# Last expert's rows kept in SBUF and placed by a 0/1 product; the other rows fetched and partly summed under it

## The chip, the cores and the metric

One core of a Trainium2 chip runs the whole program. The metric is the device time of one execution in microseconds (us), the median of several. A profile is one further execution with the hardware profiler on; its own time stands beside it. TensorE is PE in the profile, VectorE is DVE, ScalarE is ACT, GpSimd is POOL and SyncE is SP.

## The reference, cut to what matters

A trunk of two layers over 1024 tokens of width 1024, all in float32. Each layer has an attention mixer, a residual with layer norm, and then a mixture of experts with its own residual and layer norm. What matters here is the second half:

```python
g_sel = argmax(g_logits)                       # one group of 8 experts of 32
top_val, top_idx = lax.top_k(e_logits, 2)      # two experts in the group
weights = g_gate * softmax(top_val)
# each (token, expert) pair:
h = silu(xb @ w_gate[e]) * (xb @ w_up[e])      # 1024 -> 512, twice
out = h @ w_down[e]                            # 512 -> 1024
y = segment_sum(out * row_w, row_tok)          # two weighted rows a token
x = layer_norm(ALPHA * x + y, gain, bias)      # ALPHA = 4 ** 0.25
```

Every token has two pairs, so there are 2048 expert rows of 4 KB in a layer.

## The kernel before, in words

Tokens lie in 8 tiles of 128 (one token a partition). The program is five blocks: attention of layer 0, experts of layer 0, attention of layer 1, experts of layer 1, and a last one. At the end of a block all engines meet at a barrier, and GpSimd clears the semaphores of the block that has ended. `Block()` is opened in `open_block`.

**Experts** (`Moe.run`). A block of 128 slots is computed for each of the 32 experts, one after the other. For expert `e`, GpSimd gathers the tokens' rows by an indirect DMA (`gather`, L1698), TensorE turns them, and three products follow: gate, up, down. Each is made of three passes of fp32r products (high part by high part, low by high, high by low), so the 2 MB of each weight matrix is split by ScalarE into a high part (L1848) and by VectorE into a low part (L352). `Moe.run`'s functions `step` hold one expert's work for each engine, and the engines work through them in order. The result goes from PSUM banks 6 and 7 to `res` (L1881 on ScalarE, L1953 on VectorE), and GpSimd sends it by an indirect DMA (`scatter`, L1703) to `o_dram` (`expert_rows`), where a token's two rows lie side by side. An expert with more than 128 tokens would have further blocks (`extra_blocks`, `more`); with these inputs there are none (64 gathers and 64 scatters in all), but what finds them out is computed: `plan_extras` at expert 30, `mark_extras` on VectorE at expert 31, `list_extras` on TensorE behind the last down product, and `keep_extras` on VectorE behind that. Only then do the engines test the count. Behind its last scatter's landing, and behind that test, GpSimd gives `rows_sent`, and SyncE fetches tile 0's rows (`first_rows`).

**Sum and norm** (`Combine`). For layer 0 it is the opening of the next attention block, for layer 1 a block of its own. For a tile `t` SyncE fetches the first rows (L2007) and the second rows (L2008), 512 KB each; it holds four tiles and asks for `t` when tile `t-2` has landed (`sync`). The rows x1 (the residual) are fetched earlier, under the last expert (L1995), four tiles of them in layer 0 and all eight in layer 1. Then:

- ScalarE scales the first rows by their weight into PSUM (L2072).
- VectorE adds the second rows with their weight (L2081), and then ALPHA times x1 (L2086).
- VectorE takes the moments (L989 to L992), ScalarE a square root (L997), VectorE the scale (L1002, L1003), ScalarE normalises (L1009).
- GpSimd multiplies by the gain (L1013) and adds the bias (L1017).
- SyncE writes the tile (L2059). In layer 1 tile 7 doesn't go through GpSimd: VectorE does its gain and bias (L2099, L2103).

In layer 0, VectorE and ScalarE first split three weight slices of the next attention (`split_w`). TensorE turns each finished tile (L343), ScalarE and VectorE split the turned tile (`keep_tile`: L348, L352), and TensorE starts the attention's projections (`first_halves`, L643) when tiles 0 to 3 have been kept; tiles 4 to 7 and the other halves follow. Matrices of plain float32 are multiplied nowhere in `Combine`; `ident` is a 128x128 float32 identity, used for turning.

## Time and profile before

| what | value |
|---|---|
| runs | 2459.29, 2459.82, 2468.2 us; median 2459.82 |
| the profiled execution's own time | 2462.13 us |
| its span in the profile | 2460.4 us |
| mean granted TensorE clock | 0.961 of 2.4 GHz |
| PE busy | 2277.2 us (93%) |
| DVE busy | 1797.3 us (73%) |
| ACT busy | 1363.2 us (55%) |
| POOL busy | 248.0 us (10%) |

Busy shares are of the span. The 1.7 us between span and time lie around the first and the last recorded instruction. TensorE's clock has two levels here, 1.2 and 2.4 GHz, which the profile writes as 0.50 and 1.00. In the page's 40 slices, counted from 0, TensorE is busy 9 tenths or more in nearly all. The low ones are slice 18 (1107 to 1168 us, the end of layer 0's experts and the opening of its sum and norm, 4 tenths), slice 19 (7 tenths) and slice 39 (2398 to 2460 us, the sum and norm of layer 1, 0).

### The profile page before, as it was taken

Reading aid. Unit: us, or ns where it says so; the run is one execution under the profiler, and the core shown is the slowest. Engines: PE = TensorE matmul, PEld = TensorE weight load, DVE = VectorE, ACT = ScalarE, POOL = GpSimd, SP = SyncE. Lnnn points to the kernel's source line nnn. Section 1 sums busy time; section 2 is a strip of 40 time slices with the busy share of each in tenths; the row PEclk is TensorE's granted clock in tenths of the full one; section 3 lists DMA queues with packets and bytes.
Section 4 is the critical chain, followed back from the end, with each engine's and each line's share of the span. In section 5 each row is a group of like instructions: output and inputs, shape, how many; then the busy total and the mean of one; then the engine's idle time right before and its main releaser. Section 6 shows DMA issues by size and latency. Waiting matters only on the chain. (4 is left out here: it accounts for less than half of the span.)

```text
span 2460.4 us, 33859 instructions
## 1 busy us (share of the span) xinstructions
PE 2277.2 (93%) x12788; PEld 1873.8 (76%) x12788; DVE 1797.3 (73%) x2520; ACT 1363.2 (55%) x1662; POOL 248.0 (10%) x238
## 2 busy tenths in 40 slices
PE   8999998989999999994799999989989999999990
PEld 6767886878888888883678778867778888888870
DVE  4665556568999999996555555556579999999986
ACT  3454435026777777773344444443047777777753
POOL 0000000001111111111400000000011111111105
PEclk9999999989999999996899999999999999999995
DMA  4010004229999999997311111105069999999975
GB/s 130 24 30 27 27 15 143 86 99 368 391 378 383 382 385 384 386 356 251 138 46 37 37 37 38 37 35 183 26 230 405 392 400 392 385 381 373 376 283 209
DMA packets 155146, 534.31 MB, mean 217 GB/s; under 512 B 39232, under 2 KB 79192, under 8 KB 105832
## 3 DMA queue, kind: packets, MB, share of 16 engines
q1 hardware_dynamic: 136208, 498.45, 53.9%
q0 software_dynamic: 18432, 33.60, 3.6%
q8 instruction: 105, 1.72, 0.3%
q14 instruction: 57, 0.47, 0.1%
q10 hardware_dynamic: 344, 0.08, 0.0%
HBM read 515.21 MB, written 50.39 MB: 230 GB/s over the span
## 5 line engine op out<-in xcount | busy, mean ns | idle before, releaser
L352 DVE TENSOR_TENSOR arena<-arena,arena 128x2048 fp32r<-128x2048 f32 (+1 forms) x458 | 955.2, 2116 | 76.9 <-ACT arena L1848 56.6
L1848 ACT CAST arena<-arena 128x2048 fp32r<-128x2048 f32 x384 | 716.1, 1917 | 134.9 <-PE psum L1625 120.1
L1625 PE MATMUL psum<-arena,arena 128*128 128x512 f32 x3072 | 734.2, 395 | 0.0
L1625 PEld LDWEIGHTS psum<-arena,arena 128*128 128x128 f32 x3072 | 569.6, 189 | 114.6 <-issue 0.4
L643 PE MATMUL psum<-arena,arena 128*128 128x512 f32 x2016 | 506.0, 401 | 8.3 <-DVE arena L352 7.6
L643 PEld LDWEIGHTS psum<-arena,arena 128*128 128x128 f32 x2016 | 369.7, 189 | 102.0 <-issue 16.2
L1636 PE MATMUL psum<-arena,arena 128*128 128x512 f32 x1536 | 365.1, 394 | 2.8 <-DVE arena L352 2.8
L1636 PEld LDWEIGHTS psum<-arena,arena 128*128 128x128 f32 x1536 | 291.6, 190 | 66.5 <-DVE arena L352 4.3
L352 DVE TENSOR_TENSOR arena<-psum,arena 128x512 fp32r<-128x512 f32 (+1 forms) x186 | 161.2, 874 | 106.3 <-ACT arena L768 55.2
L785 ACT ACTIVATE arena<-arena,arena 128x640 f32<-128x640 f32 (+4 forms) x192 | 120.0, 626 | 202.8 <-DVE arena L883 152.3
L343 PE MATMUL psum<-ident,arena 128*128 128x128 f32 x1024 | 151.0, 289 | 64.3 <-POOL arena L1017 26.7
L343 PEld LDWEIGHTS psum<-ident,arena 128*128 128x128 f32 x1024 | 145.6, 196 | 81.2 <-POOL arena L1017 31.6
L1168 PE MATMUL psum<-arena,arena 128*128 128x512 f32 x768 | 194.7, 410 | 8.5 <-ACT arena L348 6.8
L737 ACT COPY arena<-psum 128x512 f32<-128x512 f32 (+3 forms) x288 | 119.8, 467 | 116.9 <-PE psum L674 116.3
L1168 PEld LDWEIGHTS psum<-arena,arena 128*128 128x128 f32 x768 | 148.7, 198 | 40.8 <-issue 7.2
L1698 POOL DMA_INDIRECT arena<-x_rows,slot_rows x64 | 97.9, 1530 | 505.8 <-DMA expert_rows<-arena,slot_rows 437.6
L674 PE MATMUL psum<-ident,arena 128*128 128x128 f32 x888 | 131.0, 277 | 16.1 <-ACT arena L737 10.9
L674 PEld LDWEIGHTS psum<-ident,arena 128*128 128x128 f32 x888 | 105.7, 141 | 44.8 <-ACT arena L737 14.7
L696 PE MATMUL psum<-arena,arena 128*64 128x128 f32 x1776 | 127.2, 283 | 0.0
L883 DVE CUSTOM_DVE_ANT_0 arena<-psum,arena 128x640 f32<-128x640 f32 (+3 forms) x192 | 104.9, 572 | 28.1 <-PE psum L662 27.7
L1703 POOL DMA_INDIRECT expert_rows<-arena,slot_rows x64 | 63.9, 998 | 545.2 <-DVE arena L1953 520.4
L662 PE MATMUL psum<-arena,arena 64*128 64x320 f32 (+5 forms) x1056 | 114.6, 336 | 2.5 <-DVE arena L883 1.3
(166 smaller groups left out, 1548.4 us busy)
## 6 DMA issues: line engine op xcount, KB each, us to landing
arena<-in_moe_w_gate SPq DMA_DIRECT2D x128, 1024.0 KB, 8.5
arena<-in_moe_w_up SPq DMA_DIRECT2D x128, 1024.0 KB, 7.7
arena<-in_moe_w_down SPq DMA_DIRECT2D x128, 1024.0 KB, 6.9
arena<-expert_rows SPq DMA_DIRECT2D x32, 512.0 KB, 5.3
x_rows<-arena SPq DMA_DIRECT2D x24, 512.0 KB, 2.7
arena<-x_rows SPq DMA_DIRECT2D x24, 512.0 KB, 7.2
arena<-in_c_w_in SPq DMA_DIRECT2D x24, 512.0 KB, 4.2
arena<-in_x SPq DMA_DIRECT2D x16, 512.0 KB, 7.3
```

The lines of the kernel that those rows point to most:

```text
L343: m = pe.transpose(dst_bank[:, j * P:(j + 1) * P], rows[:, c0 + j:rows.shape[1]:stride], ident[:])
L352: return eng.tensor_tensor(tile, src, high.bitcast(F32), ALU.subtract)
L643: mm = pe.matmul(job_bank(i, g), w[:, c * P:(c + 1) * P], xs[:, c, half_cols(g)], start=(a == 0), stop=(a == 23))
L662: done[h] = pe.matmul(psum[:, at:at + w], qs[b][own, t * P:(t + 1) * P], ks[kv][own, k0 + a:k0 + a + w], start=(k == 0), stop=(k == 2))
L674: mm = pe.transpose(bank(B_TURN + h)[:, (b - 4 * g) * P:(b - 4 * g + 1) * P], probs_of(s, h)[:, b * P:(b + 1) * P], ident[:])
L696: mm = pe.matmul(bank(B_OUT)[DH * h:DH * (h + 1), (t % 4) * P:(t % 4 + 1) * P], v_r[pair.kv][:, (kt + b) * P + DH * h:(kt + b) * P + DH * ...
L737: copy(probs_t[s % 2][h][:, a:b], bank(B_TURN + h)[:, 0:b - a]).then_inc(t_copied[h], 1)
L785: act.activation(probs_a[s % 2][h][:, 0:ahead + nk], biased[h][:, 0:ahead + nk], ACT.Exp, bias=low[s % 2][h], scale=-1.0, accum_out=rowsum ...
L1168: return pe.matmul(bank(2 * (t % 2) + half), ys[:, c, t * P:(t + 1) * P], w[:, c, half * BANK:(half + 1) * BANK], start=(k == 0 and c == 0 ...
L1625: mm = pe.matmul(bank(o), cs[:, c * P:(c + 1) * P], ws[:, c * FF:(c + 1) * FF], start=(k == 0 and c == 0), stop=(k == 2 and c == CH - 1))
L1636: mm = pe.matmul(bank(B_Y + s), hs[:, c * P:(c + 1) * P], ws[:, c * D + s * BANK:c * D + (s + 1) * BANK], start=(k == 0 and c == 0), stop= ...
L1848: act.copy(w_hi[w][:, cols], self.raw[w][:, cols]).then_inc(hi_ready[w], 1)
```

## The change

Seven things are altered, in both layers unless said.

1. **The last expert's rows stay.** Expert 31's result is not copied to `res` and not scattered. ScalarE multiplies each half of it, straight from PSUM, by the weight of each slot (`w_slot`) into `tail_hi` (fp32r), and VectorE forms `tail_lo`, the product less the high part. The first half is released by the down product before its second half (`half_done`).
2. **A 0/1 matrix a tile.** `pick_tokens` (VectorE, at expert 30) writes `picks`: for a slot of expert 31 and a token, 1 where the token is the slot's.
3. **Weights by slot.** The 2048 pair weights are written to DRAM at expert 6 (`w_dram`), and one indirect DMA (behind expert 10's scatter) fetches those of expert 31's slots. `clear_last` fills expert 31's rows in `o_dram` with zeros at the start.
4. **Rows are fetched under the last expert.** SyncE fetches tiles 0 to 6 from when expert 30's rows have landed, each into a place of its own. Tile 7's follow when the last expert's rows are in `tail`. In layer 0 the residual's tiles 4 to 7 come behind those.
5. **Sums ahead.** Under the last down product, ScalarE scales the first rows of tiles 0 to 2 and VectorE finishes tiles 0 and 1 (rows and residual); tile 2 is finished in the next block.
6. **TensorE adds.** `sum_up(t)`: `picks` by `tail_hi` and `tail_lo` for every tile, and for tiles 3 to 7 before that the identity by the first and by the second rows, both scaled by ScalarE and both plain float32. Layer 1 has four pairs of banks for it, layer 0 two. VectorE then has one addition of 1024 columns a tile instead of two.
7. **Around it.** `Block(no_gpsimd_drain=True)`. The extra blocks are found out only where the count isn't zero. The square root's table is loaded at the end of the experts. In layer 1 tile 3 too is ended on VectorE. In layer 0 the three weight slices are split inside the loop over tiles.

The core of the diff (what is left out names semaphores, moves buffers, and rewrites the extra blocks, which don't run here):

```diff
-            return ctx2.enter_context(nc.Block())
+            return ctx2.enter_context(nc.Block(no_gpsimd_drain=True))
...
+                            if half_done is not None and k == 2 and s == 0:
+                                mm.then_inc(half_done, 1)
...
                     for e in range(EXPERTS - 2):
+                        if e == 6:
+                            sp.wait_ge(before.weights_ready, 1)
+                                sp.dma_start(w_dram.rearrange("(t p k) o -> p k (t o)", p=P, k=2), w_pair[:]
+                                             ).then_inc(w_sent, 16)
...
+                    sp.wait_ge(lo_ready[UP], 1 + 2 * EXPERTS)
+                    combine.rows_ahead(sp, 0)
+                    sp.wait_ge(y_out[0], 8 * EXPERTS)
+                    sp.wait_ge(y_out[1], 8 * EXPERTS)
+                    sp.wait_ge(xt_ready, 1 + EXPERTS)
+                    combine.fetch_rows(sp, 0)
+                    sp.wait_ge(up_done, 1 + EXPERTS - 1)
+                    combine.fetch_rows(sp, 1)
+                    sp.wait_ge(up_done, 1 + EXPERTS)
+                    combine.fetch_rows(sp, 2)
+                    sp.wait_ge(gate_done, 1 + EXPERTS)
+                    combine.fetch_rows(sp, 3)
+                    sp.wait_ge(lo_ready[DOWN], 1 + 2 * EXPERTS)
+                    combine.rows_ahead(sp, 1)
+                    for t in range(4, TILES - 1):
+                        combine.fetch_rows(sp, t)
...
+                    sp.wait_ge(tail_lo, 2)
+                    combine.last_rows(sp)
...
+                    def clear_last():
+                        pool.memset(res[1], 0.0).then_inc(cleared, 1)
+                        pool.memset(w_slot, 0.0).then_inc(cleared, 1)
+                        pool.wait_ge(cleared, 2)
+                        scatter(res[1], slot_rows[:, LAST, 1:2], y_out[1])
...
-                        act.wait_ge(down_done, 1 + e + 1)
                         act.wait_ge(res_free, e + 1)
-                        act.copy(res[b][:, 0:BANK], bank(B_Y)).then_inc(y_act, 1)
+                        if not last:
+                            act.wait_ge(down_done, 1 + e + 1)
+                            act.copy(res[b][:, 0:BANK], bank(B_Y)).then_inc(y_act, 1)
+                            return
+                        combine.scale_first(act, 0)
+                        combine.scale_first(act, 1)
+                        act.wait_ge(x_rows_in, 16)
+                        for s in range(2):
+                            act.wait_ge(down_done, ALL_DOWN - 1 + s)
+                            act.mul(tail[0][:, s * BANK:(s + 1) * BANK], bank(B_Y + s), w_slot).then_inc(tail_hi, 1)
+                        combine.scale_first(act, 2)
...
+                    act.activation(stats[:, 0, 19:20], ident[:, 0:1], ACT.Sqrt)
...
                             before.plan_extras(dve)
+                            pick_tokens()
                         else:
-                            before.mark_extras(dve)
+                            count.append(extra_count(dve))
+                            combine.make(dve, 0)
+                            combine.make(dve, 1)
...
+                        for s in range(2):
+                            cols = slice(s * BANK, (s + 1) * BANK)
+                            dve.wait_ge(tail_hi, s + 1)
+                            dve.scalar_tensor_tensor(out=tail[1][:, cols], in0=bank(B_Y + s), scalar=w_slot,
+                                                     in1=tail[0][:, cols].bitcast(F32), op0=ALU.mult,
+                                                     op1=ALU.subtract).then_inc(tail_lo, 1)
...
+                    def pick_tokens():
+                        chain.link(dve.tensor_copy(last_token, slot_rows[:, LAST, 0:1]))
+                        chain.link(dve.tensor_scalar(token_in, tile_from[:], last_token, None, ALU.add))
+                        for t in range(TILES):
+                            dve.tensor_scalar(picks[:, t * P:(t + 1) * P], iota_cols[:], token_in[:, t:t + 1], None,
+                                              ALU.is_equal)
...
+                whole = (3, TILES - 1) if last else ()
+                write_order = (0, 1, 3, 2, 4, 5, 7, 6) if last else range(TILES)
+                    return bank(2 * (t % 4), 2) if last else bank(2 + 2 * (t % 2), 2)
...
-                def scale_first(act, t):
-                    self.rows_here(act, t)
-                    if t >= 2:
-                        act.wait_ge(added, t - 1)
-                    act.mul(sum_banks(t), firsts[t % 4], w_pair[:, 0, t:t + 1]).then_inc(scaled, 1)
+                def sum_up(pe, t):
+                    if t >= pairs_of_banks:
+                        pe.wait_ge(added, t - pairs_of_banks + 1)
+                    if t >= MADE:
+                        self.was_scaled(pe, t)
+                    pick = self.picks[:, t * P:(t + 1) * P]
+                    for s in range(2):
+                        cols = slice(s * BANK, (s + 1) * BANK)
+                        into = sum_banks(t)[:, cols]
+                        if t >= MADE:
+                            pe.matmul(into, ident[:], firsts[t][:, cols], start=True, stop=False)
+                            pe.matmul(into, ident[:], seconds[t][:, cols], start=False, stop=False)
+                        pe.matmul(into, pick, self.tail_hi[:, cols], start=(t < MADE), stop=False)
+                        mm = pe.matmul(into, pick, self.tail_lo[:, cols], start=False, stop=True)
+                    mm.then_inc(summed, 1)
...
-                    if not last:
-                        for i in range(3):
-                            split_w(i)
-                    scale_first(act, 0)
+                    self.scale_both(act, 3)
+                    self.scale_both(act, 4)
                     for t in range(TILES):
-                        if t + 1 < TILES:
-                            scale_first(act, t + 1)
                         if t >= 1:
                             act_norm(act, t - 1)
+                        if 1 <= t < TILES - 4:
+                            self.scale_both(act, t + 4)
+                        if not last and t in (1, 2):
+                            split_w(t - 1)
...
-                    for t in range(4):
+                    for t in range(3):
                         turn_tile(t)
+                        sum_up(pe, t + 5)
+                    turn_tile(3)
                     first_halves(0)
```

How instructions stand now, at the places that matter. SyncE behind its last weights, in layer 1, before (numbers of `arena` are places in SBUF; the first eight here hold the residual's tiles):

```order
L1670 DMA arena_72<-in_ln_gain 128x1024
L1670 DMA arena_72<-in_ln_bias 128x1024
L1995 DMA arena_19082<-x_rows 128x1024
...
L1995 DMA arena_19089<-x_rows 128x1024
L1598 TENSOR_LOAD plan
```

and after:

```order
L2126 DMA arena_19226<-x_rows 128x1024
L2138 DMA arena_19199<-expert_rows 128x1024
L2139 DMA arena_19207<-expert_rows 128x1024
...
L2138 DMA arena_19202<-expert_rows 128x1024
L2139 DMA arena_19210<-expert_rows 128x1024
L2126 DMA arena_19227<-x_rows 128x1024
L2126 DMA arena_19228<-x_rows 128x1024
L2126 DMA arena_19229<-x_rows 128x1024
L2126 DMA arena_19230<-x_rows 128x1024
L2138 DMA arena_19203<-expert_rows 128x1024
L2139 DMA arena_19211<-expert_rows 128x1024
```

Fourteen fetches of rows have come in front of the test of the count: those of tiles 0 to 3 between the residual's two halves, those of tiles 4 to 6 behind them.

VectorE from expert 30's end to the last expert's end, in layer 1, after (19233 is `picks`, 19199 to 19201 are the first rows of tiles 0 to 2, 19207 and 19208 the second rows, 19223 and 19224 the residual, 19231 and 19232 `tail_hi` and `tail_lo`):

```order
L2074 TENSOR_SCALAR arena_19233<-iota_cols,arena_19292 128x128 x8
L2058 COPY arena_19282<-psum 128x512
L357 TENSOR_TENSOR arena_19195<-arena_19189,arena_19192 128x2048 x2
L2037 TENSOR_TENSOR arena_19285<-arena_19284,psum 128x512
L357 TENSOR_TENSOR arena_19287<-psum,arena_19286 128x512
L1614 TENSOR_LOAD plan
L1614 ISA x2
L2178 SCALAR_TENSOR_TENSOR arena_19199<-arena_19207,w_pair,arena_19199 128x1024
L2183 SCALAR_TENSOR_TENSOR arena_19199<-arena_19223,arena_19199 128x1024
L2178 SCALAR_TENSOR_TENSOR arena_19200<-arena_19208,w_pair,arena_19200 128x1024
L2183 SCALAR_TENSOR_TENSOR arena_19200<-arena_19224,arena_19200 128x1024
L2065 SCALAR_TENSOR_TENSOR arena_19232<-psum,arena_19290,arena_19231 128x512 x2
```

The picks stand in front of the copy of expert 30's result, and four passes over tiles 0 and 1 stand where `mark_extras` was, in front of the low part of the tail.

TensorE in the last block, where it had nothing before (tile 2's four products, then tile 3's first half; 19202 and 19210 are tile 3's rows):

```order
L2259 MATMUL psum<-arena_19231,arena_19233 128x512
L2260 MATMUL psum<-arena_19232,arena_19233 128x512
L2259 MATMUL psum<-arena_19231,arena_19233 128x512
L2260 MATMUL psum<-arena_19232,arena_19233 128x512
L2257 MATMUL psum<-arena_19202,ident 128x512
L2258 MATMUL psum<-arena_19210,ident 128x512
L2259 MATMUL psum<-arena_19231,arena_19233 128x512
L2260 MATMUL psum<-arena_19232,arena_19233 128x512
```

Tiles 0 to 2 have four products each, tiles 3 to 7 eight, half of them by the float32 identity.

## Rows read from the trace of the kernel before

**Rows 1.** The timeline, layer 1's end: start us, length, engine, line, count.

```profile
2380.21 0.69 DVE L1953 COPY arena<-psum 128x512 f32<-128x512 f32 x1
2381.74 0.97 POOL L1703 DMA_INDIRECT expert_rows<-arena,slot_rows  x1 [16.18 <-DVE arena L1953]
2382.81 4.49 DVE L352 TENSOR_TENSOR arena<-arena,arena 128x2048 fp32r<-128x2048 f32 x2 [1.91 <-ACT arena L1848]
2390.11 8.66 PE L1636 MATMUL psum<-arena,arena 128*128 128x512 f32 x24 [1.40 <-DVE arena L352]
2400.33 0.97 POOL L1703 DMA_INDIRECT expert_rows<-arena,slot_rows  x1 [17.62 <-DVE arena L1953]
2404.43 0.32 SPq L2007 DMA_DIRECT2D arena<-expert_rows  x1
2410.09 1.12 ACT L2072 ACTIVATE psum<-arena,w_pair 128x1024 f32<-128x1024 f32 x1 [10.70 <-PEq L2214]
2410.44 0.42 SPq L2008 DMA_DIRECT2D arena<-expert_rows  x1
```

**Rows 2.** The chain of work that ended last: start us, length, what.

```profile
2411.80 6.50 DMA arena<-expert_rows
2422.83 2.35 POOL arena L1013
2453.63 2.38 POOLq L2214
```

**Rows 3.** The timeline, one tile's work in layer 1's last block.

```profile
2428.65 1.22 DVE L2086 SCALAR_TENSOR_TENSOR arena<-arena,psum 128x1024 f32<-128x1024 f32 x1
2430.23 1.24 ACT L1009 ACTIVATE arena<-arena,stats 128x1024 f32<-128x1024 f32 x1 [2.02 <-DVE stats L1003]
2431.38 1.10 ACT L2072 ACTIVATE psum<-arena,w_pair 128x1024 f32<-128x1024 f32 x1
2431.74 1.28 DVE L2081 SCALAR_TENSOR_TENSOR psum<-arena,w_pair,psum 128x1024 f32<-128x1024 f32 x1
2433.05 1.22 DVE L2086 SCALAR_TENSOR_TENSOR arena<-arena,psum 128x1024 f32<-128x1024 f32 x1
```

**Rows 4.** Windows of layer 1's end: stretch, length, busy of five engines, PEclk, DMA share, GB/s.

```profile
2384.00:2388.00 4.00, 1.34 (x7) 0.80 (x5) 3.90 (x3) 0.59 (x1) 0.00 (x0) 1.00 0.07 26
2416.00:2420.00 4.00, 0.00 (x0) 0.00 (x0) 2.51 (x2) 1.92 (x3) 0.00 (x0) 0.50 1.01 409
```

**Rows 5.** The timeline, end of layer 0 and opening of layer 1's attention.

```profile
1144.96 2.94 ACT L756 CAST arena<-arena 128x1024 fp32r<-128x1024 f32 x3 [10.88 <-PEq L2214]
1176.34 1.22 DVE L2086 SCALAR_TENSOR_TENSOR arena<-arena,psum 128x1024 f32<-128x1024 f32 x1
1182.18 1.22 DVE L2086 SCALAR_TENSOR_TENSOR arena<-arena,psum 128x1024 f32<-128x1024 f32 x1
1186.94 7.81 PE L643 MATMUL psum<-arena,arena 128*128 128x512 f32 x24 [4.49 <-DVE arena L352]
1212.18 16.61 PE L643 MATMUL psum<-arena,arena 128*128 128x512 f32 x72 [1.55 <-DVE arena L352]
```

**Rows 6.** The timeline, products by the float32 identity (two records each).

```profile
528.40 3.15 PE L1122 MATMUL psum<-ident 128*128 128x128 f32 x26
544.36 4.62 PE L1122 MATMUL psum<-ident 128*128 128x128 f32 x20
```

**Rows 7.** Windows of 1 us, PE alone: busy, PEclk, DMA share, GB/s.

```profile
1175.00:1176.00 1.00, 1.00 (x7) 0.50 1.04 426
2395.00:2396.00 1.00, 1.00 (x4) 0.50 0.02 8
```

**Rows 8.** Groups by form, 0/1 rows on VectorE: count | busy, mean ns.

```profile
L1390 DVE TENSOR_SCALAR arena<-iota_cols,arena 128x128 f32<-128x128 f32 x32 | 9.0, 283 | 0.3
```

**Rows 9.** The DMA view, 405 to 420 us: packets, and an issue's size and landing.

```profile
DMA packets 6164, 2.68 MB, mean 179 GB/s; under 512 B 5552, under 2 KB 5552, under 8 KB 6162
```

**Rows 10.** Waits, 600 to 1100 us: total, times, longest.

```profile
ACT arena L1848 <- PE psum L1625: 56.5, 56, 1.3
```

308 lines of the change are left out of this document (205 added, 103 removed).

## The prediction, made before the changed kernel ran

> **What bounds the kernel now.** I read the page's busy slices first. They show TensorE nearly full everywhere but at the two sums and norms, so a change there counts in full, and one under the experts counts only where it delays TensorE. The waits of the expert stage say the same: ScalarE's weight splits wait for TensorE, not for a DMA [rows 10].
>
> Then the timeline of layer 1's end [rows 1]. The last down product ends at 2398.8, the last scatter is issued at 2400.3, the first fetch of rows follows 4.1 us later, and ScalarE starts the last block at 2410.1. The chain of waits [rows 2] goes through the landing of tile 2's rows at 2418.3 to GpSimd, which starts at 2422.8 and then never stops: it ends its seventh tile at 2456.0, 33.2 us later, 4.74 a tile. The last write lands with the span's end, 4.4 us behind. So the end is set by when GpSimd starts, how many tiles it has, and whether it must pause.
>
> Layer 0's end is the same 1265.1 us earlier (1144.96 against 2410.09) [rows 1, 5], but there VectorE has most to do, a tile in 5.84 us (its second additions at 1176.34 and 1182.18). TensorE's first projection waits for VectorE until 1186.9, and the attention proper starts at 1212.2 [rows 5].
>
> **The change part by part.**
>
> *Under the experts.* The picks are 8 instructions of 0.283 us [rows 8] and two small ones of some 0.2: 2.6 us in front of the copy at 2380.21, which then ends at 2383.5. The low split of the last down weights behind it began at 2382.81 [rows 1], so the last expert gets 0.7 us later, in each layer. Expert 30's scatter moves from 2381.7 to 2384.3. The zero fill and the weights' fetch stand on GpSimd, idle for most of an expert (16 to 17 us ahead of a scatter) [rows 1]; I take them at nothing. The 2048 weights of 4 bytes go by SyncE's queue at expert 6. The nearest row is the router's load: 5552 packets under 512 B within some 15 us, along with larger ones [rows 9], so 2048 need at most 6 us of a queue, and nobody waits for a DMA there. I take 0.3 us for both layers; the bounds are 0 and 6 each.
> The Trainium skill (DMA: Bandwidth & Descriptors, Specifications) says that below 512 B the DMA engine does a read-modify-write. No row here shows a 4-byte write; by that rule I would sooner go to the upper bound.
>
> *Rows under the last expert.* Moved past on SyncE's queue: the residual's second half (layer 0: two weight slices) now stands behind tiles 0 to 3 and behind the wait for expert 30's scatter, which ends after the other waits there. Its first reader is tile 4's addition, over 30 us later, so I count nothing. Fetches start at 2384.3 + 4.1 = 2388.4, into a DMA that is all but idle (share 0.07 in 2384 to 2388) [rows 4]. A tile's pair of 1.05 MB takes 2.6 us at the 409 GB/s of a full queue [rows 4]; 2.7 taken. Tile 2's pair landed 6.5 us from issue with another ahead of it [rows 2], which leaves 1.3 of start-up. Tile 0 lands at 2388.4 + 0.9 (issue) + 1.3 + 2.6 = 2393.2, tile 3 at 2401.3, and tile 4, behind the residual's 2 MB, at 2409.4. Tiles 0 and 1 are scaled and made (1.10, then 1.28 + 1.22 each [rows 3]) by 2399.4, beside the down product, which ends at 2399.5; the tail's low part then ends at 2401.
>
> *The barrier.* TensorE's listing of extra blocks, the last scatter and its landing go. Before, 5.7 us passed from SyncE's start of the first fetch to ScalarE's first work behind the barrier (2404.43 to 2410.09) [rows 1]. With no GpSimd drain I take under 1 us behind the last engine, which is ScalarE: tail's high part 2400.1, tile 2's scaling 2401.2, test of the count, table and root 1.5 us; the block opens at 2404.0. Bounds: 2403, and 2409.5 if the whole 5.7 us stays. In layer 0, SyncE has four fetches more and I take 1139.6.
>
> *Layer 1.* GpSimd's start now needs tile 0's root, which on ScalarE stands behind the scaling of tile 4: 2409.4 + 2 x 1.1 = 2411.6, root 0.2, VectorE's scale 0.4, normalise 1.24 [rows 3], with gaps 2414.0 (before 2422.8). Three tiles take it to 2428.2. Now VectorE is late: ScalarE's rounds of 4.2 us (2 x 1.1, 0.2, 1.24 and VectorE's scale between) give tile 3's root at 2424, two passes of 1.28 end it at 2426.7, and moments of tile 4, addition of tile 5 and tile 4's scale and normalise bring tile 4 to GpSimd at 2431.5: a pause of 3.3. Three more tiles: 2445.7 against 2456.0, a gain of 10.3.
>
> *TensorE's additions.* A float32 identity product of 128 columns is two records: 26 in 3.15 us at 2.4 GHz and 20 in 4.62 at 1.2 [rows 6], so 0.24 and 0.46 us. Of 512 columns none is in the trace. Bounds: the price of an fp32r product, 0.23 (16.61 / 72) [rows 5], and four times 0.24. I take four times, 0.97, since the record's length goes with columns; a tile of 3 to 7 then costs 4 x 0.97 + 4 x 0.23 = 4.8 us at 2.4 GHz and 9.2 at 1.2. In layer 1 four pairs of banks let TensorE run on from tile 0 without a stop, so it is at the high level within tile 3 (in [rows 1] 24 products took 8.66 from a low start) and ends each tile before VectorE asks.
> The Trainium skill (FP8 and Floating Point Precision, TensorE Precision Notes) has true FP32 as four passes; the trace agrees (0.24 against 0.06 for a quarter of 0.23).
>
> *Layer 0.* TensorE's turns of tiles 0 to 3 and the projections now queue behind the sums of tiles 4 to 7, and these behind VectorE's additions two tiles back. VectorE loses 1.28 a tile and gets the three splits (1.2 each) inside the loop, where ScalarE has 2.2 us of scaling and 1.05 of splitting in the first rounds. Laying the four engines' programs against each other by hand with the durations above, the additions of tiles 0 to 7 end at 1143.4, 1146.5, 1153.9, 1161.3, 1168.3, 1173.0, 1179.3, 1184.0. Before, tile 7's was at 1189.2 (1182.18 + 5.84 + 1.22) [rows 5]. The start of the block gains 5.4, and what the loop gains and pays cancels out; the gain handed to the attention is 5.2.
>
> *Sum.* -10.3 - 5.2 + 0.3, and 1 us for engines that load code behind the jump over the extra blocks (unseen; 0 to 5.7, the barrier's bound) = -14.2. The profiled execution's 2462.1 (span 2460.4 and 1.7 around it) becomes 2447.9. It stood 2.3 above the median, so for the median 2459.8 - 14.2 = 2445.6.
>
> **The rivals.**
>
> *The barrier stays long.* The profile puts the release down to TensorE, not GpSimd [rows 1, 5]. For it: the releaser. Against it: the two layers' 5.7 and 5.6 us fit an end of GpSimd's own. Blocks open at 2409.5 and 1145.1: layer 1 gains 6, layer 0 nothing, in all 2454.
>
> *DMA is slower.* Up to nine tiles' worth are queued at once. At 3.4 us a pair tile 4 lands 5 us later: 5.3 and 2.3 gained, 2452.5. Against it stands the 409 GB/s.
>
> *Layer 0's clock swings.* There two pairs of banks make TensorE wait for VectorE at every tile. If it falls to 1.2 GHz in each gap, a tile costs some 7 us and layer 0 gains 1: 2449.7. For it: brief work in gaps stayed at 0.50 (1175) [rows 7]. Against: the new work fills over three quarters of the time.
> The Trainium skill (TensorE: Matmul & The Clock Gate, A second HAM failure mode: psum-queue depth-cycling) describes just that, small idle times between groups that cycle through banks; by it the sum is 2449.7.
>
> *Slower.* TensorE stays at 1.2 GHz through all additions, as it did in layer 0's turns [rows 7]. At 9.2 us a tile it passes GpSimd's 4.74 and VectorE's round, and the sum of tile 7 sets both ends: by the same timetables layer 0 ends 7.3 and layer 1 4.5 later than before, with the 1.3 above 2473. It turns slower once a tile costs over 7.9 us in both layers. Against: in [rows 1, 7] solid work of 6 us raised the clock (0.50 still at 2395, the 24 products over in 8.66 where all at 1.2 GHz would need over 10).
>
> *It does not do what it says* (the landings come too late for the sums ahead, and tail and barrier wait for them): only with a pair over 4 us; 2457.
>
> *Everything fits.* 2.56 us a pair, full clock from tile 3 in layer 0: 11.2 and 7.7, 2441.
>
> **How the numbers follow.** Forecast 0.50; barrier 0.12, DMA 0.09, swinging clock 0.10, slower 0.05, too late 0.04, everything fits 0.10. Time 2445.6, the forecast's own range 2443 to 2449. The range 2440 to 2455 leaves out the slow case and the worst ends. A measurement of this kernel can tell about 0.5% from no change, 12.3 us, so "faster" begins at 2447.5. Of the forecast three quarters lie below (0.38), all of "everything fits" (0.10), and 0.06 of the others: 0.54. Slower 0.06, same 0.40.
>
> **What would show it.** In the profile after: the last down product 0.7 us later; rows fetched from about 10 us ahead of its end; 3 to 5 us from it to the last block's first work; GpSimd's first gain at 2414 less layer 0's 5, six tiles with a pause of some 3 us in the middle; float32 products of some 0.43 us a record at 2.4 GHz; layer 0's addition of tile 7 some 5 us earlier. Wrong would be: a block that opens more than 7 us behind the down product, VectorE's additions waiting for TensorE in layer 1, PEclk at 0.50 beyond tile 4 in either layer, or expert rounds longer than before.

## The result: 0.4% slower, and the profile after

| | before | after |
|---|---|---|
| median of 12 runs each, beside one another | 2462.38 us | 2471.69 us |
| lowest, highest | 2457.28, 2468.2 | 2469.94, 2476.17 |
| profiled execution, its span | 2462.13, 2460.4 | 2471.77, 2469.8 |

The ratio is 1.0041, with a 95% interval of 1.0031 to 1.0050. By the bound of 0.5% in the prediction this is "the same"; by the interval it is slower. The 2445.6 forecast is missed by 26 us, and the range (to 2455) by 17.

I compared the traces stage by stage, by the start of GpSimd's scatters and of TensorE's products. The two run together to within 0.3 us up to expert 5's scatter in layer 0 (673.31 and 673.20). Then:

| stretch | shift at its end | made in it | predicted |
|---|---|---|---|
| layer 0, experts 6 and 7 (scatter 1082.09, now 1089.59) | +7.5 | +7.5 | +0.15 |
| layer 0's end (attention proper 1212.18, now 1222.55) | +10.4 | +2.9 | -5.2, code +1 |
| attention of layer 1 (a scatter 1884.70, now 1896.99) | +12.3 | +1.9 | 0 |
| layer 1, experts 6 and 7 (2364.58, now 2384.28) | +19.7 | +7.4 | +0.15 |
| layer 1's end (span) | +9.4 | -10.3 | -10.3 |

So layer 1's end came out as forecast, and the loss lies in three places where I had counted nothing or a gain: the two stalls (14.9 where I had 0.3), layer 0's end (2.9 where I had -4.2) and the attention (1.9 where I had 0). Together that is 23.6 us, the whole miss of the span (+9.4 for -14.2).

**Where the experts stall.** First SyncE's queue in the timeline of after, at expert 6 (start us, length, line), then ScalarE and TensorE:

```profile
661.76 0.65 SPq L1690 DMA_DIRECT2D pair_weights<-w_pair  x1
664.18 6.65 SPq L1566 DMA_DIRECT2D arena<-in_moe_w_up  x2
670.88 6.75 SPq L1566 DMA_DIRECT2D arena<-in_moe_w_gate  x2
...
682.68 1.90 ACT L1929 CAST arena<-arena 128x2048 fp32r<-128x2048 f32 x1 [4.65 <-DMA arena<-in_moe_w_up]
...
681.51 2.10 PE L1645 MATMUL psum<-arena,arena 128*128 128x512 f32 x8
689.00 7.53 PE L1656 MATMUL psum<-arena,arena 128*128 128x512 f32 x24 [5.39 <-DVE arena L357]
```

The two pairs of issues behind the write, which took 3.17 and 2.53 us at this place in before, take 6.65 and 6.75; I read that as a queue that takes no more. ScalarE now waits for a DMA there, where [rows 10] showed it waiting for TensorE alone, and TensorE stands still for 5.4 us and restarts at the low clock (PEclk 0.50 from 688 to 692). The windows of before and after (last two columns: DMA share, GB/s) show what the queue carried:

```profile
668.00:672.00 4.00, 4.00 (x23) 3.45 (x22) 4.00 (x3) 2.27 (x4) 0.00 (x0) 1.00 0.99 410
672.00:676.00 4.00, 4.00 (x19) 3.30 (x18) 2.98 (x3) 4.00 (x3) 1.00 (x1) 1.00 1.01 419
676.00:680.00 4.00, 4.00 (x20) 3.30 (x19) 4.00 (x4) 3.25 (x3) 0.00 (x0) 1.00 1.00 370
```

```profile
668.00:672.00 4.00, 4.00 (x23) 3.45 (x22) 4.00 (x3) 2.23 (x4) 0.00 (x0) 1.00 0.89 61
672.00:676.00 4.00, 4.00 (x20) 3.28 (x19) 2.94 (x3) 2.59 (x2) 1.00 (x1) 1.00 0.54 36
676.00:680.00 4.00, 4.00 (x19) 3.34 (x18) 2.85 (x2) 1.91 (x1) 0.00 (x0) 1.00 0.78 139
684.00:688.00 4.00, 0.00 (x0) 0.00 (x0) 2.29 (x1) 2.74 (x3) 1.48 (x1) 0.74 1.02 427
```

In these 12 us the queues moved 3.9 MB less than in before, about 9.4 us at 410 GB/s. TensorE is still full while the rate is low (column 3). Its gap opens at 683.6, some 15 us after the rate fell and 3 after it had recovered, which is why the cause has to be looked for ahead of the stall.

**Layer 0's end.** The timeline of after, SyncE's queue, ScalarE, GpSimd, VectorE and TensorE:

```profile
1135.13 6.23 SPq L314 DMA_DIRECT2D arena<-in_c_w_in  x2
1141.40 3.39 SPq L2138 DMA_DIRECT2D arena<-expert_rows  x1
1149.40 2.54 SPq L2126 DMA_DIRECT2D arena<-x_rows  x4
...
1152.45 4.27 ACT L2156 ACTIVATE arena<-arena,w_pair 128x1024 f32<-128x1024 f32 x4 [7.44 <-PEq L2421]
...
1160.95 2.37 POOL L1023 TENSOR_TENSOR arena<-arena,arena 128x1024 f32<-128x1024 f32 x1 [32.22 <-ACT arena L1019]
1169.63 2.36 POOL L1023 TENSOR_TENSOR arena<-arena,arena 128x1024 f32<-128x1024 f32 x1 [3.88 <-ACT arena L1019]
...
1163.85 2.98 DVE L357 TENSOR_TENSOR arena<-arena,arena 128x1024 fp32r<-128x1024 f32 x1 [2.70 <-ACT arena L766]
...
1222.55 12.80 PE L653 MATMUL psum<-arena,arena 128*128 128x512 f32 x55 [1.56 <-DVE arena L357]
```

ScalarE was done at 1145.0 and waited 7.44 us for the barrier. The releaser named is TensorE's queue, but the last to come was SyncE, whose last issue ended at 1151.94, 0.5 ahead of the opening. Then GpSimd, which never paused for tiles 0 to 2 in before, stands idle 3.88 us behind tile 0, because VectorE first waits 2.70 us for ScalarE's cast of a weight slice and then takes 2.98 over its split.

**Layer 1's end.** The timeline of after; these lines answer to [rows 1 to 3]:

```profile
2421.70 1.03 SPq L2139 DMA_DIRECT2D arena<-expert_rows  x1
...
2423.53 2.19 ACT L2156 ACTIVATE arena<-arena,w_pair 128x1024 f32<-128x1024 f32 x2 [2.14 <-PEq L2421]
2429.82 2.19 ACT L2156 ACTIVATE arena<-arena,w_pair 128x1024 f32<-128x1024 f32 x2 [4.10 <-DMA arena<-expert_rows]
...
2433.98 2.37 POOL L1023 TENSOR_TENSOR arena<-arena,arena 128x1024 f32<-128x1024 f32 x1 [28.32 <-ACT arena L1019]
2452.44 2.35 POOL L1023 TENSOR_TENSOR arena<-arena,arena 128x1024 f32<-128x1024 f32 x1 [2.23 <-ACT arena L1019]
2464.31 2.34 POOL L1027 TENSOR_TENSOR arena<-arena,arena 128x1024 f32<-128x1024 f32 x1
```

Less the 19.7 us of shift, GpSimd starts at 2414.3 (forecast 2414.0) and ends at 2446.9 (2445.7), with one pause of 2.2. Its third tile takes 1.9 us longer than the others (passes of 3.34 and 3.23 where 2.35 is usual), beside VectorE's work on tile 3. That the span's gain is 10.3 to the tenth is luck: GpSimd ends 9.1 us earlier than in before, not 10.3, and the span ends 3.2 us behind it where it was 4.4.

### The profile page after: what moved, and what is told of

It reads as the page before. It is cut to its first block and busy times, and to the rows that moved or that the text cites. A ratio compares the mean times of both kernels' runs of the same rounds, so it can differ in the third digit from the quotient of the medians.

```text
span 2469.8 us, 34012 instructions
## 1 busy us (share of the span) xinstructions
PE 2324.0 (94%) x12868; PEld 1895.1 (77%) x12868; DVE 1788.7 (72%) x2499; ACT 1374.6 (56%) x1675; POOL 273.1 (11%) x243
## 5 line engine op out<-in xcount | busy, mean ns | idle before, releaser
L348 PE MATMUL psum<-ident,arena 128*128 128x128 f32 x1024 | 147.4, 284 | 31.0 <-DMA arena<-x_rows,slot_rows 14.2
L1748 POOL DMA_INDIRECT arena<-x_rows,slot_rows x64 | 113.5, 1774 | 505.9 <-DMA expert_rows<-arena,slot_rows 461.7
```

Source lines behind the costliest of these rows:

```text
L348: m = pe.transpose(dst_bank[:, j * P:(j + 1) * P], rows[:, c0 + j:rows.shape[1]:stride], ident[:])
```

## Experiments

All ran beside the kernel before; its medians lay between 2460.1 and 2462.5. "Packed" below is the kernel of the first experiment. In the first four, one thing is changed.

**1. Weights in 64-byte pieces.**

```diff
-    sp.dma_start(w_dram.rearrange("(t p k) o -> p k (t o)", p=P, k=2), w_pair[:]
+    sp.dma_start(w_dram.rearrange("(p k t) o -> p k (t o)", p=P, k=2), w_pair[:]
...
+    chain.link(dve.tensor_scalar(at_w, token, 127, 4, ALU.bitwise_and, ALU.arith_shift_left))
+    chain.link(dve.tensor_scalar(at_k, pair, 1, 3, ALU.bitwise_and, ALU.arith_shift_left))
+    chain.link(dve.tensor_scalar(at_t, token, 7, None, ALU.arith_shift_right))
...
-    in_offset=bass.IndirectOffsetOnAxis(ap=slot_rows[:, LAST, 1:2],
+    in_offset=bass.IndirectOffsetOnAxis(ap=at_w, axis=0),
```

> The changed kernel, with the 2048 weights of each layer written to DRAM as 128 pieces of 64 bytes (a layout by partition; five small VectorE operations work out where the last expert's weights then lie). SyncE's wait ahead of the write and its place at expert 6 are kept. Theory, the 4-byte pieces block the DMA queues: the trace of after shows 61, 36 and 139 GB/s in 668:672, 672:676 and 676:680 where before has 410, 419 and 370, and each layer is 7.4 us late behind it, so both stalls go: 15 us less than after, 2457, which is 5 less than before. Rival, SyncE's wait for VectorE's weights or the fetch of the weights by GpSimd makes the stall: nothing changes, 2471 to 2472. Second rival, the size of the piece matters less than the 8 KB write in front of the weights: half goes, 2464.

Measured: 2455.83 us, ratio 0.9975 (0.9966 to 0.9985), so 15.9 less than after, and a little below before (by less than 0.5%, so "the same" by the prediction's bound). That is the theory. The dip is gone (mean of 664 to 680 us: 395 GB/s, in after 152, in before 394), and the write lands 8.6 us behind its issue where it took 17.3:

```profile
668.00:672.00 4.00, 4.00 (x20) 3.33 (x20) 4.00 (x3) 1.84 (x2) 1.15 (x1) 1.00 0.98 391
672.00:676.00 4.00, 4.00 (x22) 3.39 (x21) 2.71 (x4) 4.00 (x5) 1.00 (x1) 1.00 1.02 419
676.00:680.00 4.00, 4.00 (x19) 3.33 (x18) 4.00 (x2) 3.31 (x2) 0.00 (x0) 1.00 0.98 376
```

SyncE's wait and the fetch are still there. The write's form is the cause of the first and the fourth line of the table. This also bares layer 0's end: the down product starts at 1125.99 (before: 1125.78), the block opens at 1144.86, and the attention proper starts at 1214.82, still 2.6 late.

**2. The write alone, in the kernel before.**

```diff
+    sp.wait_ge(w_ready, 1)
+    sp.dma_start(w_dram.rearrange("(t p k) o -> p k (t o)", p=P, k=2), w_pair[:]).then_inc(w_sent, 16)
```

> The kernel before, with one thing added: the write of the 2048 weights in 4-byte pieces at expert 6 of each layer, which nothing reads (GpSimd fetches nothing from it). Theory, the 4-byte pieces block the queues by themselves: 7.4 us a layer, 15 in all, 2477 where before has 2462, and the same dip of GB/s at 668:680. Rival, it is the sum of the write with GpSimd's fetch of the weights, with the fill of the last expert's rows or with the picks: 2462 to 2465.

Measured: 2475.05 us, ratio 1.0060 (1.0043 to 1.0077), the theory. The traced run was the fastest of four (2467.95): experts 6 and 7 took 7.3 us more in layer 0 and 3.5 in layer 1, so the size varies.

**3. The two projection slices fetched behind the jump.** The lines go from `rows_ahead` to the next block's `sync`:

```diff
-                if group == 1 and not self.last:
-                    for i in range(2):
-                        fetch_job(sp, 1, i)
...
                     if not last:
+                        for i in range(2):
+                            fetch_job(sp, 1, i)
                         sp.wait_ge(added, 1)
```

> The changed kernel, with the two fetches of layer 1's projection weights that stand on SyncE ahead of tiles 4 to 7's rows (6.23 us of issue at 1135.13) moved behind the jump to the next block. Theory, the block behind the experts of layer 0 opens 0.5 us behind SyncE's last issue: it opens near 1146.5 in place of 1152.45, and as the additions there hang on it, the attention of layer 1 starts 4 to 6 us sooner: 2466 to 2468 where after has 2471.7. Rival, the rows of tiles 4 to 7 bound it: their fetches start sooner too, so they'd give the same start but the gain would stop at tile 4: 1 to 2 us. Second rival, the projection weights land late for ScalarE's split and hold the attention: nothing, or up to 3 us slower.

Measured: 2467.86 us, ratio 1.0023 (1.0013 to 1.0032). The median is in the theory's range, but the trace does not bear the theory out in full. The block opened at 1148.85, 2.3 us later than forecast (0.4 of it because the stage itself ran later), and then:

```profile
1148.83 13.08 SPq L314 DMA_DIRECT2D arena<-in_c_w_in  x3
...
1163.75 1.04 ACT L766 CAST arena<-arena 128x1024 fp32r<-128x1024 f32 x1 [4.46 <-DMA arena<-in_c_w_in]
```

The slices landed late behind the rows, GpSimd's first pause grew from 3.88 to 6.71 us, and the attention started at 1221.82. Counted from the down product's start (1133.33, in after 1132.89), 4.0 us were gained at the opening and 1.2 were left at the attention. So SyncE's queue does set the opening, and the second rival takes most of it back. The median shows more (3.8) than the trace; the traced run was that kernel's slowest.

**4. GpSimd's drain put back.**

```diff
-            return ctx2.enter_context(nc.Block(no_gpsimd_drain=True))
+            return ctx2.enter_context(nc.Block())
```

> The changed kernel, with the drain of GpSimd at the end of every block put back as before had it. Theory, the barrier was 11 us long in before because of it (ScalarE's wait of 10.7 us behind the experts of layer 1): each expert block's successor opens 4 to 6 us later, 8 to 12 in all, 2480 to 2484. Rival, the barrier got short because GpSimd had less to do behind its last scatter and the drain costs nothing: 2471 to 2473.

Measured: 2469.72 us, ratio 1.0034 (1.0021 to 1.0046), no slower than after. The trace shows a price in layer 1 only:

```profile
2423.57 1.50 SPq L2139 DMA_DIRECT2D arena<-expert_rows  x1
...
2428.83 2.19 ACT L2156 ACTIVATE arena<-arena,w_pair 128x1024 f32<-128x1024 f32 x2 [5.55 <-PEq L2421]
```

The block opens 3.8 us behind SyncE's last issue, against 0.8 in after; in layer 0 it is 0.4 against 0.5. By the trace the drain is worth 3 us, in layer 1 alone, not the 8 to 12 I had given it. The medians show no price at all (this kernel's is 2.0 below after's), and its runs spread by 8.6.

**5. VectorE's weight splits one tile later, in packed** (packed is the base of 6, 7 and 9 too). In `vector`:

```diff
-                        if not last and t in (1, 2):
-                            split_w(t - 1)
+                        if not last and t in (2, 3):
+                            split_w(t - 2)
```

> The kernel with the weights written in 64-byte pieces, in which VectorE splits the first two projection weights behind the additions of tiles 2 and 3 instead of 1 and 2 (ScalarE's casts stay). Theory, layer 0's end is late because VectorE waits 2.70 us for ScalarE's cast and then takes 2.95 us for a weight split ahead of each of two tiles' additions, which leaves GpSimd idle for 3.89, 3.89 and 1.77 us: with VectorE not waiting there, the first gap and most of the second go and layer 1's attention starts 5 to 7 us sooner, 2449 to 2451 where that kernel has 2455.8. Rival, the order only moves the gaps, as VectorE is full from tile 3 on (5.84 us a tile in before): 0 to 2 us. Second rival, the gaps come from TensorE's float32 additions of tiles 3 and 4: nothing changes.

Measured: 2446.29 us, ratio 0.9952 (0.9938 to 0.9966). GpSimd goes through the first tiles:

```profile
1149.10 2.38 POOL L1023 TENSOR_TENSOR arena<-arena,arena 128x1024 f32<-128x1024 f32 x1 [31.47 <-ACT arena L1019]
1153.89 2.37 POOL L1023 TENSOR_TENSOR arena<-arena,arena 128x1024 f32<-128x1024 f32 x1
1160.15 2.37 POOL L1023 TENSOR_TENSOR arena<-arena,arena 128x1024 f32<-128x1024 f32 x1 [0.59 <-ACT arena L1019]
...
1204.48 16.66 PE L653 MATMUL psum<-arena,arena 128*128 128x512 f32 x72 [1.56 <-DVE arena L357]
```

From the opening (1140.59) to the attention are 63.9 us, in packed 70.0: the 6 us of the theory, from an edit that removes no work. The median fell by 9.5, more than this stretch explains; experiment 10 comes back to that.

**6. Both: fetches behind the jump as in 3, and in `scalar` and `vector` both splits at tile 3.**

```diff
-                        if not last and t in (1, 2):
-                            split_w(t - 1)
+                        if not last and t == 3:
+                            split_w(0)
+                            split_w(1)
```

> The kernel with the weights written in 64-byte pieces; the two fetches of projection weights stand behind the jump into layer 0's last block, and ScalarE and VectorE split both at tile 3. Theory: the block opens 3.6 us sooner, as it did where only the fetches moved (1148.85 against 1152.45), the weights have landed by the time tile 3 asks for them (15 us behind the opening), and GpSimd goes through tiles 0 to 2 without a gap: 8 to 10 us less than 2455.8, 2446 to 2448. Rival, the weights land late again and hold ScalarE at tile 3: 2452 to 2457.

Measured: 2446.18 us, ratio 0.9940 (0.9927 to 0.9954). Opening at 1137.30, attention at 1202.98; the two splits in a row leave GpSimd a pause of 5.88 us ahead of tile 3. Counted from the down product's start, the attention comes 2.5 us sooner than in experiment 5 (80.2 and 82.7 us), but the medians show no difference.

**7. Rows fetched only behind the last down product.**

```diff
                     sp.wait_ge(y_out[1], 8 * EXPERTS)
+                    sp.wait_ge(down_done, ALL_DOWN)
```

The edit does a second thing that is not shown: ScalarE's scaling and VectorE's sums of tiles 0 and 1 move behind the last expert's own rows, as they must when their rows come late.

> The kernel with the weights written in 64-byte pieces, with all fetches of rows for the sums held until the last expert's down product has ended, and tiles 0 and 1 scaled and summed behind the last expert's own rows. The last expert's rows still stay on chip. Theory, fetching under the last expert carries the change's gain at layer 1's end and about as much at layer 0's: SyncE has some 10 us of issue left behind the down product, and the blocks open 6 to 9 us later: 2468 to 2474 where that kernel has 2455.8. Rival, keeping the last expert's rows on chip carries it: 2456 to 2460.

Measured: 2476.83 us, ratio 1.0063 (1.0047 to 1.0079), 21 more than packed. The blocks opened at 1157.04 and 2430.21, where packed had 1144.86 and 2408.70: 12.2 us later in layer 0 and another 9.3 in layer 1. With the last expert's rows kept on chip but the other rows neither fetched nor summed ahead, this kernel is 16 us slower than before. So the gain hangs on the work ahead; how much of it is the fetching and how much the sums, this run does not separate.

**8. Half the pieces, in the kernel before.**

```diff
+    half = w_dram[0:PAIRS // 2, :].rearrange("(t p) o -> p (t o)", p=P)
+    sp.dma_start(half, w_pair[:, 0, :]).then_inc(w_sent, 16)
```

> The kernel before, with one thing added: the write of 1024 weights (one of the two sets) in 4-byte pieces at expert 6 of each layer, which nothing reads. In the changed kernel 2048 pieces cost about 3.85 MB of other transfers (9.6 us at 400 GB/s), of which 7.4 us reach the end. Theory, the prefetched weights absorb the first 2 us: half the pieces block 4.8 us and cost 2 to 3 a layer, 2466 to 2468. Rival, the price goes by the piece, with nothing absorbed: 3.7 a layer, 2469 to 2470. Second rival, a threshold: with 1024 the prefetch covers it all, 2461 to 2463.

Measured: 2470.62 us, ratio 1.0044 (1.0030 to 1.0057), 10 us over before, where all 2048 cost 13 to 15. That is above the theory and just above the first rival. The traced run, one of the faster ones (2468.29), lost 4.3 us at experts 6 and 7 of layer 0 and 1.7 in layer 1. That is 6.0 in all, against 10.8 in experiment 2's traced run, so by the traces half the pieces cost a little over half and by the medians three quarters. This run alone does not tell whether the price goes by the piece.

**9. As 6, but with `if not last and t in (2, 3): split_w(t - 2)` on both engines.**

> As the kernel with both splits at tile 3 (weights in 64-byte pieces, the two projection weights' fetches behind the jump), but with the casts and splits of ScalarE and VectorE at tiles 2 and 3. Theory: that kernel opened its block 3.3 us sooner than the one with only VectorE's splits moved, and lost it in one gap of 5.88 us on GpSimd ahead of tile 3, where two splits stand in a row; spread over two tiles the gap shrinks to about 2.5 us as in the other, and layer 1's attention starts 2 to 4 us sooner: 2442 to 2444. Rival, the projection weights, which then land some 15 us behind the opening, hold ScalarE's cast at tile 2: 2446 to 2450.

Measured: 2447.96 us, ratio 0.9950 (0.9933 to 0.9968), the rival. The block opened at 1136.36, ScalarE's cast waited 1.10 us for its slice, GpSimd paused 3.89 and 5.87 us, and the attention started at 1206.69.

**10. Experiment 5 again**, with no edit to it.

> The kernel with the weights in 64-byte pieces and VectorE's splits behind tiles 2 and 3, once more, beside the one above on the same chip: 2446.3 again, within 1.5 us. A rival to the whole account would show here: that its gain over before comes from the chip or the hour of the first measurement, 2450 or more.

Measured: 2450.14 us (2444.47 to 2455.12), ratio 0.9949 (0.9931 to 0.9967). The median is 3.9 over the first time, outside the 1.5 I had given it, and by the number it is the rival's; yet the gain over before stands in both measurements, with ratios that differ by 0.0003. By this median the move of the splits is worth 5.7 us over packed, by the first 9.5. The traced executions of this one kernel differ by 12 us (spans 2441.3 and 2453.4), of which 8.6 had come up by the first expert's scatter (580.81 and 589.41). That is why single spans aren't compared here, only stretches.

**11. The 4-byte write in eight parts, one an expert, in after.**

```diff
+    if 6 <= e < 6 + TILES:
+        t = e - 6
+        sp.dma_start(w_dram[2 * t * P:2 * (t + 1) * P, :].rearrange("(p k) o -> p (k o)", k=2), w_pair[:, :, t])
```

> The changed kernel (2471.7), with the 4-byte write cut into eight writes of 256 weights, one an expert from expert 6 to 13; GpSimd fetches them at expert 16. The number and the size of the pieces are the same. In the changed kernel the write takes about 9.6 us of transfer from the queues at once. Theory, the stall comes from the burst: 256 pieces take 1.2 us, and as the queues carried 354 GB/s of the 410 to 425 that they can (6.29 MB in 17.76 us an expert), each expert has some 2 us to spare, so both stalls go: 2456 to 2459. Rival, each 4-byte piece costs the queues its time whenever it comes, or SyncE's issue is held longer by each write: 2468 to 2472.

Measured: 2608.97 us, ratio 1.0597 (1.0582 to 1.0612). 137 us slower than after, which falls outside both forecasts. Each part of 256 pieces dug its own hole; this is the first:

```profile
668.00:672.00 4.00, 4.00 (x20) 3.30 (x19) 3.73 (x3) 3.34 (x2) 2.16 (x1) 1.00 1.35 379
672.00:676.00 4.00, 4.00 (x23) 3.46 (x22) 3.52 (x3) 2.88 (x4) 0.48 (x1) 1.00 1.11 82
676.00:680.00 4.00, 4.00 (x19) 3.30 (x19) 3.42 (x3) 2.72 (x2) 0.53 (x1) 1.00 0.57 65
```

The scatters of experts 6 to 13 come 22 to 32 us behind the one before, not 17.8. SyncE's issue of a part took 0.5 to 0.7 us, so the issue is not what held the queue. The first hole is 6.7 us of transfers, where 2048 pieces at once made one of 9.4, and the parts cost 8.6 us of the end each: cutting the write multiplied its price. What 256, 1024 and 2048 share is the layout: sixteen pieces, from eight or sixteen partitions, in each 64 bytes of DRAM.

**12 to 14. Spacing, in the kernel before.** 12 writes 2048 pieces 64 bytes apart, 13 writes 128 dense, 14 writes the same 128, 64 bytes apart:

```diff
-    w_dram = nc.dram_tensor("pair_weights", [PAIRS, 1], F32).ap()    # experiment 2
+    w_dram = nc.dram_tensor("pair_weights", [PAIRS, 16], F32).ap()   # 12: column 0 written
+    w_dram = nc.dram_tensor("pair_weights", [P, 1], F32).ap()        # 13
+    w_dram = nc.dram_tensor("pair_weights", [P, 16], F32).ap()       # 14: column 0 written
+    sp.dma_start(w_dram[:, 0:1], w_pair[:, 0, 0:1]).then_inc(w_sent, 16)   # 13, 14
```

> The kernel before, with a write of all 2048 weights in 4-byte pieces at expert 6 that nothing reads, each piece 64 bytes from the next in DRAM (where the dense layout puts sixteen pieces, from sixteen partitions, into 64 bytes). Theory L, pieces that fall into the same 64 bytes are written one behind the other, which takes as long for 16 such pieces as for 128 rows of them (256, 1024 and 2048 dense pieces all blocked the queues for 8 to 9 us): the dip of GB/s goes, and 2461 to 2464. Rival F, a write in 4-byte pieces has a fixed price of 7 us whatever its layout: 2474 as with the dense write alone. Rival N, it is the number after all: 2474 too, with the 128-piece kernels at 2462.

> The kernel before, with a write of 128 weights (one a partition, one tile) in 4-byte pieces at expert 6, dense: eight runs of 64 bytes, sixteen pieces in each. Theory L (pieces in the same 64 bytes follow one another): as dear as 2048, 7 us a layer, 2473 to 2476. Rival F (a fixed price of the form): the same. Rival N (the number of pieces): nothing to see, 2460 to 2463.

> The same write of 128 weights, each piece 64 bytes from the next. Theory L: the dip goes, 2460 to 2463, where the dense one has it. Rival F: 2473 to 2476 as dense. Rival N: 2460 to 2463, and the dense one too.

Measured: 2462.59 (ratio 1.0001, 0.9989 to 1.0012), 2462.32 (0.9999, 0.9988 to 1.0010) and 2461.73 us (1.0004, 0.9994 to 1.0015). None moves the end. The rates tell more, in the order 12, 13, 14:

```profile
668.00:672.00 4.00, 4.00 (x20) 3.29 (x19) 3.71 (x2) 3.72 (x2) 2.14 (x1) 1.00 0.83 206
672.00:676.00 4.00, 4.00 (x23) 3.45 (x22) 3.56 (x4) 2.50 (x4) 0.05 (x1) 1.00 0.81 148
```

```profile
672.00:676.00 4.00, 4.00 (x23) 3.46 (x22) 3.56 (x4) 2.27 (x5) 0.00 (x0) 1.00 0.99 107
676.00:680.00 4.00, 4.00 (x20) 3.29 (x19) 3.42 (x3) 3.40 (x2) 1.00 (x1) 1.00 0.76 243
```

```profile
672.00:676.00 4.00, 4.00 (x19) 3.27 (x19) 2.98 (x4) 4.00 (x4) 1.00 (x1) 1.00 1.02 423
676.00:680.00 4.00, 4.00 (x19) 3.32 (x18) 4.00 (x4) 3.25 (x3) 0.00 (x0) 1.00 0.98 374
```

The mean rate of 664 to 680 us puts all the writes on one scale, by one traced execution of each. The last column is what the queues carried less than in before, as time at 410 GB/s:

| write at expert 6 of layer 0 | GB/s | transfers lost |
|---|---|---|
| none (before) | 394 | |
| 128 pieces of 64 bytes (packed) | 395 | none |
| 128 pieces of 4 bytes, 64 bytes apart (14) | 388 | 0.2 us |
| 2048 of 4 bytes, 64 bytes apart (12) | 285 | 4.3 us |
| 128 of 4 bytes, dense (13) | 277 | 4.6 us |
| 256, dense (11, the first part) | 223 | 6.7 us |
| 1024, dense (8) | 228 | 6.5 us |
| 2048, dense (2; after has 152) | 161 | 9.1 us |

So number and layout both count, and by much the same: sixteen times the pieces cost 4 to 5 us at either layout, and the dense layout costs 4 to 5 at either number. Neither theory L nor rival N is right as it was written: L had the dip of 12 gone (it halved) and 13 as dear at the end as 2048 pieces, N had 12 as dear as the dense write and nothing to see in 13 (its time fits, its dip does not). Rival F, a fixed price, is out by 12 and 14. Some 2 to 4 us of a dip are absorbed by the weights already fetched (13 lost 4.6 us of transfers and its next expert came 0.7 us late; experiment 2 lost 9.1 and came 7.3 late in layer 0); beyond that TensorE pays. Whether 64 bytes is the width that matters wasn't tried.

## Why the prediction was wrong, point by point

Two of the signs that the prediction had named for being wrong came: expert rounds longer than before (24.9 and 18.7 us at experts 6 and 7 of layer 0, usually 17.8), and a block that opens more than 7 us behind the down product (12.2 in layer 0; 6.5 in layer 1).

- **"2048 need at most 6 us of a queue, and nobody waits for a DMA there. I take 0.3 us for both layers."** This step failed, and it is the one that turned the sign: the term that I put at 0.3 measured 14.9 us in the table, 15.9 by experiment 1, 13 by experiment 2. Two errors. The row behind "at most 6" [rows 9] showed reads of small pieces (the router's weights), which say nothing on writes. And "nobody waits for a DMA" was read from a stage in which the queue never faltered [rows 10]; it ran at 384 GB/s on average (620 to 980 us of before), of which 354 are weights (6.29 MB in 17.76 us), and the fullest windows show some 425, so it had little to give. My own bounds, 0 and 6 each, held the sum at 2457.3 at most.
  The Trainium skill (DMA: Bandwidth & Descriptors, Specifications) has transfers below 512 B as read-modify-write. It pointed to the right side and I did not follow it. The runs go further than the rule: pieces of 64 bytes are below it too and cost nothing, and pieces of 4 bytes cost nothing that reaches the end where they lie 64 bytes apart.
- **Layer 0, "the block opens at 1139.6".** In packed, which is free of the stall, it opened at 1144.86, 5.3 late. The barrier itself was short, as forecast (0.5 us behind the last engine). I had counted SyncE's fetches at issue price; two of them took 6.23 us, since the queue in front was full of rows. Experiment 6, which has these two behind the jump, opens 4.4 us sooner when counted from the down product's start. Moving a fetch past others costs its blocked issue, and a barrier waits for SyncE too.
- **Layer 0, "the three splits (1.2 each) inside the loop"; "what the loop gains and pays cancels out".** The split took 2.98 us beside GpSimd, and VectorE waited 2.70 for the cast, with the next tile's addition queued behind. The additions in packed end 5.3 late at tile 0 and 7.2 late at tile 7, so the loop costs 2 more. Experiment 5 gives back 6. That its 2446.3 and 2450.1 lie near the 2445.6 that was meant for this kernel is in part luck: it opens as late as packed and makes up for it with an order of splits that I had not counted on.
- **"1 us for engines that load code behind the jump".** No run shows it. The blocks open 0.5 us (layer 0) and 0.8 us (layer 1) behind SyncE's last issue. The sums of three rivals (2454, 2452.5 and 2441) leave this 1 us out, too small a slip to change a chance.
- **Layer 1's end, -10.3.** Right, and near its own steps, though equal to the tenth by luck, as said above: tile 4's rows release ScalarE at 2410.1 (shift taken off; forecast 2409.4), GpSimd starts 0.3 later, pauses 2.2 us (3.3). The picks cost nothing (0.7): the low split at 2382.81 [rows 1] came at 2402.53, exactly the shift.
- **TensorE's float32 additions.** A product of 512 columns takes 0.86 us from start to start (forecast 0.97), a tile 4.36 us, and neither end waits for them. In layer 0 the clock did fall behind a pause, as the rival of the swinging clock had it: it was low over tile 4 (PEclk 0.50 at 1168 to 1172) and full again from 1176. But no addition of VectorE waited for TensorE, so the rivals on the clock did not decide.
- **The drain.** I took the barrier's shortness to be its doing. The part that I can attribute is 3 us in the trace of layer 1 (experiment 4), and the medians don't show even that.
- **Attention of layer 1, +1.9, not in the forecast.** The last heads' products, before and after:

```profile
1651.50 1.46 PE L662 MATMUL psum<-arena,arena 64*128 64x320 f32 x12
```

```profile
1662.18 1.97 PE L672 MATMUL psum<-arena,arena 64*128 64x320 f32 x12
```

The same twelve products are slower, with 0.67 as the granted clock of 1660 to 1670 where before had 0.89 and 0.83. Packed and experiment 3 show it too (463.7 and 464.7 us from attention to output product; before 461.2), experiment 5 does not (460.8), though there too one such group takes 1.97 us (1644.11). So the low clock in these products is at most a part of it, and what sets it stays open.

## What to carry to other kernels

A small write on a queue that runs near its limit is priced by the number and the layout of its pieces, not by its bytes: lay the tensor out so that each partition writes one run (or at least keep 4-byte pieces 64 bytes apart), even at the price of a few index operations, and don't cut such a write into parts. A fetch moved ahead of others into a full queue holds the issuing engine, and so any barrier behind it. And a wait placed in front of the work that feeds the pacing engine costs its full length at every turn; moving it one tile on was worth 6 us here.

## What the runs showed of the hardware

- **Dense 4-byte writes.** 256 pieces, 1 KB in all, took the queues from some 375 to some 75 GB/s for 8 us (experiment 11); the same 2048 weights as 128 pieces of 64 bytes left no trace (experiment 1).
- **VectorE beside GpSimd.** The split of 128x1024 from SBUF takes 1.2 us by itself (three in 3.50 at layer 0's opening in before) and up to 3.3 (experiment 5) where it starts while GpSimd runs its gain or bias. The times fit a wait and not a slower run:

```profile
1163.40 2.35 POOL L1027 TENSOR_TENSOR arena<-arena,arena 128x1024 f32<-128x1024 f32 x1
```

  This pass of GpSimd ends at 1165.75, and the split shown above, started at 1163.85, ends 1.08 us later, at 1166.83, which is about its own price; in layer 1 too VectorE's pass of 3.06 us (2444.92) ends 1.08 behind GpSimd's of 3.34 (2443.56). The other way round, where a split is already running, GpSimd's bias pass grows from 2.35 to 3.23 us (1192.15 in after). Splits that read PSUM kept their 0.65 (two in 1.29 us). The Trainium skill (Trainium Architecture — The Big Picture, What this means for kernel authors) has VectorE and GpSimd share a port under an exclusive lock; the trace agrees for operations on SBUF alone.
- **The best kernel of the runs** is packed with the splits moved: ratio 0.9952 and 0.9949 to before in two measurements. Experiments 6 and 9 are level with it.
